# Float32 weights cast in every group of a hybrid encoder block, with first loads in quarters, a fixed TensorE order and a split last pass

## The reference

```python
h = rmsnorm(x, norm1_g);  p = h @ w_in            # 2560 columns: B, C, x~, u, v
y_a = B * conv3(C * x~)                            # causal depthwise, width 3
v = layernorm(v);  y_b = u * (W_s v + b_s)         # 128x128 per head, masked by chunks of 64
y = concat(rmsnorm(y_a), rmsnorm(y_b))
x = x + y @ w_out
a = relu(rmsnorm(x, norm2_g) @ w_up)
x = x + (a * a) @ w_down                           # hidden width 4096
out = rmsnorm(x, final_g)
```

## Time and profile before

| | |
|---|---|
| median of 3 runs | 1398.94 us (1398.16 to 1399.78) |
| profiled execution, its own time | 1400.48 us |
| span on its slowest core (core 2) | 1398.9 us |
| spans of the 8 cores | 1389.2 to 1398.9 us |
| TensorE matmul busy | 1307.5 us, 93% |
| VectorE, ScalarE busy | 657.2 us (47%), 608.9 us (44%) |
| HBM read, written | 138.31 MB, 40.89 MB |

### The profile page before, as it was taken

The page is one execution under the profiler, slowest core; times in us unless marked ns, Lnnn a source line. Parts: engine busy times, 40 slices in busy tenths (PEclk is TensorE's granted clock), DMA queues, the critical chain, the costliest instruction groups (busy, mean ns, idle before and its releaser), DMA issues.

```text
span 1398.9 us, 18098 instructions; the slowest of 8 cores (1389.2 to 1398.9 us)
## 1 busy us (share of the span) xinstructions
PE 1307.5 (93%) x6141; PEld 591.0 (42%) x6264; DVE 657.2 (47%) x1035; ACT 608.9 (44%) x1093; POOL 28.0 (2%) x54
## 2 busy tenths in 40 slices
PE   1789899999999989999999999999999998999995
PEld 0334344444444434444444444444444443444442
DVE  4268831311686953112378883131168694311217
ACT  2444534143465461442556453414346545144152
POOL 1100000000000000000000000000000000000000
PEclk9899999999999999999999999999999999999998
DMA  9999976651271312210255311121125131221003
GB/s 226 174 179 207 194 190 165 140 146 60 95 267 61 121 61 83 99 61 30 82 195 179 148 61 61 60 104 48 61 103 198 61 120 61 82 100 61 1 1 121
DMA packets 39243, 156.26 MB, mean 112 GB/s; under 512 B 2288, under 2 KB 15728, under 8 KB 33520
## 3 DMA queue, kind: packets, MB, share of 16 engines
q1 hardware_dynamic: 20432, 130.98, 26.2%
q0 software_dynamic: 18720, 24.12, 11.9%
HBM read 138.31 MB, written 40.89 MB: 128 GB/s over the span
## 4 chain that ended last, share of the span: by engine, by line
PE 86%; DVE 5%; DMA 5%; issue 2%; ACT 1%; POOL 0%; DVEq 0%; SPq 0%; ACTq 0%; POOLq 0%
PE PS L358 86%; DMA RING<-w_in 4%; DVE HT L449 4%; DMA X<-xT 1%; DVE SACC L437 0%; DVE X L449 0%; ACT SQF L432 0%; DVE ATY L449 0%; ACT RS L417 0%; ACT RS L419 0%; POOL RING L374 0%; DVE YA L561 0%; DVE SSUM L437 0%; DVE X L612 0%; DVE YA L553 0%
## 5 line engine op out<-in xcount | busy, mean ns | idle before, releaser
L358 PE MATMUL PS<-HT,RING 128*128 128x512 bf16 x3005 | 683.8, 383 | 34.0 <-DVE HT L449 19.3
L358 PE MATMUL PS<-ATY,RING 128*128 128x512 bf16 x2509 | 559.3, 379 | 4.9 <-DVE ATY L449 1.5
L358 PEld LDWEIGHTS PS<-HT,RING 128*128 128x128 bf16 x3072 | 300.7, 99 | 399.5 <-issue 48.8
L649 DVE TENSOR_TENSOR X<-PS,X 128x512 f32<-128x512 f32 x256 | 176.2, 691 | 535.7 <-PE PS L358 535.7
L358 PEld LDWEIGHTS PS<-ATY,RING 128*128 128x128 bf16 x2560 | 250.0, 98 | 303.6 <-issue 2.6
L633 ACT ACTIVATE RL<-PS 128x512 f32<-128x512 f32 x256 | 151.6, 596 | 429.7 <-PE PS L358 428.5
L636 ACT ACTIVATE ATY<-RL 128x512 bf16<-128x512 f32 x256 | 158.2, 629 | 19.0 <-ACT RL L633 0.8
L432 ACT ACTIVATE SQF<-X 128x512 f32<-128x512 f32 x168 | 103.2, 626 | 125.5 <-DVE X L612 49.3
L437 DVE TENSOR_TENSOR SACC<-SACC,SQF 128x512 f32<-128x512 f32 x176 | 120.8, 687 | 45.2 <-ACT SQF L432 42.2
L449 DVE SCALAR_TENSOR_TENSOR HT<-X,PRM,RS 128x512 bf16<-128x512 f32 x128 | 86.2, 745 | 53.7 <-ACT RS L419 53.7
L358 PE MATMUL PS<-RING,HT 128*128 128x512 bf16 x252 | 63.6, 404 | 13.1 <-DVE HT L449 12.7
(11 more groups left out here) (58 smaller groups left out, 352.2 us busy)
## 6 DMA issues: line engine op xcount, KB each, us to landing
RING<-sc_up SPq DMA_DIRECT2D x12, 2048.0 KB, 7.9
RING<-sc_dn SPq DMA_DIRECT2D x12, 2048.0 KB, 7.9
X<-xT SPq DMA_DIRECT2D x32, 512.0 KB, 11.8
oT<-X SPq DMA_DIRECT2D x32, 512.0 KB, 4.3
RING<-w_up POOLq DMA_DIRECT2D x4, 2048.0 KB, 20.9
RING<-w_down POOLq DMA_DIRECT2D x4, 2048.0 KB, 21.1
sc_up<-RING SPq DMA_DIRECT2D x4, 2048.0 KB, 9.6
sc_dn<-RING SPq DMA_DIRECT2D x4, 2048.0 KB, 8.9
```

The source lines that it names most:

```text
L358: ins = e.matmul(o, lhsT=l, rhs=r, start=st, stop=sp)
L649: S.add("dve", lambda e, dc=dc, bank=bank: e.tensor_tensor(out=X[xb][:, dc, :], in0=PS[bank][:, :], in1=X[xb][:, dc, :], op=ALU.add), read ...
```

## The change

Weights are cast from float32 by GpSimd's DMA in all four groups; the bf16 copies in HBM, their write-backs and SyncE's reloads are gone. The first casts carry no tokens: V in two halves of 4 k-chunks, then eight quarters of XU and BC in the order of use, then OUT, all queued at once. SyncE sends the parameters, tile 0, and then, behind the first V half, the other small inputs; tile 1 follows behind quarter 2 of BC, and tile mA + 2 behind the first matmul group of `ffn_up(mA, 0)` (a `gate`). TensorE's large groups and GpSimd's casts keep the order of the program (`seq`); statistics matmuls alone are free to move, and have PSUM bank 7 for themselves, so 7 banks rotate. The planner's durations change, and the two rounds behind the first sort by latest start. `stage0` and `norm2` become `x_norm`. V of tile 0 is computed chunk by chunk into 4 banks, its conv stage in two halves with the halo between, and LayerNorm in two halves of two banks. The 2-column copy in `Z` moves from GpSimd to VectorE. `final(mA)` follows `ffn_down(mA, 3)`. In the last group `ffn_down(mA, 3)` and `final(mA)` come before `ffn_up(mB, 3)`, and `tail_down_final` does the last down pass in two halves of 256 tokens, with the sum of squares on ScalarE and TensorE.

```diff
-        order = run(lambda op: (op.prio, -op.bl, op.idx), 0.0)
-        if self.two_pass:
+        order = run(lambda op: (op.prio, op.idx), 0.0)
+        for _round in range(2):
...
-            order = run(lambda op: (ls[id(op)], op.idx), 0.4)
+            order = run(lambda op: (ls[id(op)], op.idx), 0.1)
...
         def alloc_bank():
-            return nxt("bank", 8)
+            return nxt("bank", 7)
+        SBANK = 7
...
-        def load_piece(i, g=1):
-            if g == 0:
-                return cast_piece_to_ring(i)
-            name, sc, src, n = pieces[i]
+        def load_piece(i):
+            src, n = pieces[i]
             slot = i % 4
-            S.add("sp", lambda e, sc=sc, slot=slot, n=n: e.dma_start(out=RING[slot][:, :, 0:n], in_=sc),
-                  reads=[("scr", i)], writes=wk(slot), dma_key=("wl", slot), nbytes=2 * 128 * 8 * n)
+            S.add("pool", lambda e: e.dma_start(out=RING[slot][:, :, 0:n], in_=src), writes=wk(slot),
+                  dma_key=("cast", i), nbytes=4 * 128 * 8 * n, seq=True)
...
+            if m == 0:
+                for k in range(8):
+                    pe_group(banks, [(PS[banks[t]][:, :], HT[:, hm, k, t * 128:(t + 1) * 128], WV[:, k, 0:512],
+                                      k == 0, k == 7) for t in range(4)],
+                             reads=[("HT", hm, k), ("Wq", 0, k // 4)])
...
+        def tail_down_final(m, p):
+            xb, hm = m % 3, m % 2
+            slot_w = (5 + 2 * p) % 4
+            WD = RING[slot_w]
+            HM = MT // 2
+            VS = VH[:].rearrange("p t (u j) -> p (t u) j", u=2)
+            for hf in range(2):
+                lo, hi = hf * HM, (hf + 1) * HM
+                for dc in range(8):
+                    bank = alloc_bank()
+                    pe_group(bank, [(PS[bank][:, 0:HM], WD[:, fc, dc * 128:(dc + 1) * 128],
+                                     AT[:, fc, hm * MT + lo:hm * MT + hi], fc == 0, fc == 7) for fc in range(8)],
+                             reads=[("ATY", fc * 2 + hm) for fc in range(8)] + wk(slot_w))
+                    S.add("dve", lambda e, dc=dc, bank=bank, lo=lo, hi=hi: e.tensor_tensor(
+                        out=X[xb][:, dc, lo:hi], in0=PS[bank][:, 0:HM], in1=X[xb][:, dc, lo:hi], op=ALU.add),
+                        reads=[("ps", bank), ("X", xb, dc)], writes=[("Xh", dc, hf)], n=HM)
+                    S.add("act", lambda e, dc=dc, lo=lo, hi=hi: e.activation(
+                        out=VS[:, dc, :], in_=X[xb][:, dc, lo:hi], func=AF.Square),
+                        reads=[("Xh", dc, hf)], writes=[("VS", dc)], n=HM)
+                for c in range(8):
+                    pe_group(SBANK, [(PS[SBANK][:, 0:HM], ONESD[:, :], VS[:, c, :], c == 0, c == 7)],
+                             reads=[("VS", c), ("const",)], seq=False, slack=0.4)
...
+                for j in range(4):
+                    store_x(m, j, lo, hi, hf)
...
-        for j, (i, q) in enumerate(((2, 0), (1, 2), (1, 0))):
-            cast_quarter(i, q, dur=w0, reads=tokv, tok=toks[j])
...
-        load_x(0)
-        load_x(1, reads=toks)
+        S.add("sp", lambda e: e.dma_start(out=PRM[:, :], in_=prm_d), writes=[("prm",)], dma_key=("misc", 0),
+              nbytes=26624)
+        load_x(0)
+        for kh in range(2):
+            cast_part(0, kh, RING[0][:, 4 * kh:4 * kh + 4, 0:512], pieces[0][0][:, 4 * kh:4 * kh + 4, :],
+                      4 * 128 * 2048)
+        for (i, q) in ((2, 0), (1, 2), (1, 0), (2, 1), (1, 3), (1, 1), (2, 2), (2, 3)):
+            cast_quarter(i, q)
+        load_piece(3)
+        late = [("Wq", 0, 0)]
+        load_x(1, reads=[("Wq", 1, 2)])
...
             for p in range(4):
-                ffn_up(mA, p)
+                ffn_up(mA, p, gate=[("gate", g, p)])
+                if p == 0 and not last:
+                    load_x(mA + 2, reads=[("gate", g, 0)])
+                if last and p == 3:
+                    ffn_down(mA, p)
+                    final(mA)
+                    ffn_up(mB, p)
+                    tail_down_final(mB, p)
+                    continue
                 ffn_up(mB, p)
...
-                if p == 3 and not last:
-                    stage0(mA + 2)
+                if p == 3:
+                    x_norm(mA + 2, G1, gate=[("gate", g, 3)])
                 ffn_down(mA, p)
+                if p == 3:
+                    final(mA)
+                    load_x(mB + 2)
                 ffn_down(mB, p)
```

More of the change, by code:

```diff
@@ L359, in fn @@
                 return ins
-            dur = 0.03 + sum(max(r.shape[-1], 64) for (_o, _l, r, _a, _b) in mms) / 2300.0
-            S.add("pe", fn, reads=reads, writes=[("ps", bank)], dur=dur, prio=prio)
+            dur = sum(0.0025 + max(r.shape[-1], 96) / 2400.0 for (_o, _l, r, _a, _b) in mms)
+            banks = bank if isinstance(bank, list) else [bank]
+            S.add("pe", fn, reads=reads, writes=[("ps", b) for b in banks] + list(gate), dur=dur, seq=seq, slack=slack)
         def wk(slot, qs=(0, 1, 2, 3)):
@@ L379, in save_piece @@
-        def save_piece(i):
-            name, sc, src, n = pieces[i]
-            slot = i % 4
-            S.add("sp", lambda e: e.dma_start(out=sc, in_=RING[slot][:, :, 0:n]),
-                  reads=wk(slot), writes=[("scr", i)], dma_key=("wsave", i), nbytes=2 * 128 * 8 * n)
-        def cast_piece_to_ring(i, dur=None, reads=(), tok=None):
-            name, sc, src, n = pieces[i]
-            slot = i % 4
-            S.add("pool", lambda e: e.dma_start(out=RING[slot][:, :, 0:n], in_=src),
-                  reads=list(reads), writes=wk(slot) + ([tok] if tok else []),
-                  dma_key=("cast", i), nbytes=4 * 128 * 8 * n, dur=dur)
-            save_piece(i)
@@ L393, in load_piece, with cast_part @@
[L393 to L399 removed]
+        def cast_part(i, q, dst, src, nb):
+            S.add("pool", lambda e: e.dma_start(out=dst, in_=src), writes=[("Wq", i % 4, q)],
+                  dma_key=("cast", i, q), nbytes=nb, seq=True)
@@ new lines, in conv_mms @@
+        def conv_mms(m, c, which):
+            hm = m % 2
+            W, off, slot, q = {"C": (RING[1], 512, 1, 2 + c // 2), "X": (RING[2], 0, 2, c // 2),
+                               "B": (RING[1], 0, 1, c // 2)}[which]
+            bank = alloc_bank()
+            pe_group(bank, [(PS[bank][:, :], W[:, k, off + c * 128:off + (c + 1) * 128], HT[:, hm, k, :],
+                             k == 0, k == 7) for k in range(8)],
+                     reads=[("HT", hm, k) for k in range(8)] + wk(slot, (q,)))
+            return bank
@@ L601, in y_norm, with add_to_x @@
             normalize(lambda c: YN[:, mm_, ebase + c, :], lambda c: src[:, c, :], gbase, 4, slot, yk,
-                      [("ATY", mm_ * 8 + ebase + c) for c in range(4)], ())
+                      [("ATY", mm_ * 8 + ebase + c) for c in range(4)])
+        def add_to_x(xb, dc, bank):
+            S.add("dve", lambda e: e.tensor_tensor(
+                out=X[xb][:, dc, :], in0=PS[bank][:, :], in1=X[xb][:, dc, :], op=ALU.add),
+                reads=[("ps", bank), ("X", xb, dc)], writes=[("X", xb, dc)])
         def out_proj(m):
```

503 lines of the change are left out of this document (222 added, 281 removed).

## The result

The changed kernel takes **1408.26 us** (median of 4 runs, 1407.23 to 1408.98) against 1398.71 us for the kernel before in the same comparison (1398.16 to 1399.78): a ratio of **1.0067**, 95% interval 1.0049 to 1.0084. It is slower by 9.5 us where 40 us less were forecast. The profiled execution has a span of 1406.9 us on core 1; the one before had 1398.9 us on core 2.

What follows compares the result with a forecast made beforehand. TensorE, busy 1307.5 of 1398.9 us, was taken as the bound, with its idle, low-clock and end times to win. Terms -10.5 - 10.3 - 3.1 - 14.4 - 2.1 = -40.4 gave 1360.1 profiled, 1359 us median; range 1341 to 1377.

Steps and rivals of the forecast that it cites:

- Casts in every group: Weight loads of all groups: float32 casts arrive in time, hidden in the FFN, XU fitting its 36 us; priced 0.
- rival 3: Group boundaries: XU's casts arrive late and stall each; slower from 49.5 us, 1416 at 55; chance 0.03.
- With that queue free tile 3 lands some 5 us of the 7 earlier.: Boundaries: OUT leaves SyncE's queue, tile 3's norm precedes its need, the 2.18 us wait goes; 4.0 a boundary.
- the -14.4: Three group boundaries together: smaller waits and clock losses, less what a fixed order loses, 3 x -4.8 us.
- The halved entry wait: FFN entry at each boundary: waits of 2.76 and 0.64 us and their clock loss halved, -2.3.
- Rival 1: Only the start pays; boundaries and group 0's FFN entry stay bound by VectorE's amount of work; 1376 us, chance 0.17.
- rival 4: Start: tile 0 lands no sooner because ten queued casts take the share; start gain 5, 1365 us, chance 0.12.
- Start, -10.5.: Before the first large matmul: tile 0 lands at 17.0, V starts at 22.5 instead of 33.06 us; -10.5.
- First stage, 42.5 us.: First token stage: weight and norm waits go, V of tile 1 at 65 instead of 83.88 us; -10.3.
- A statistics bank ... priced 0: PSUM and TensorE order: bank 7 set aside, seven rotating banks cover VectorE for 12 us; cost 0 in the FFN.
- the rest of group 0: Group 0 after its first token stage: of 7.9 us lost, 3.1 saved, for the boundaries' reason; -3.1.
- Tail, -2.1.: End: 9.3 instead of 15.8 us after the last matmul, less added work and two 1.6 us switches; -2.1.

Runs made afterwards that it cites:

- e7: Changed kernel, but OUT's cast at each group's end waits for tile mA's four stores, order replanned; 1376.1 us (die median), -22.2 against the kernel before.
- f1: Changed kernel with every engine's order kept, OUT's cast made to wait for tile mA's stores after planning; 1387.4 us (die median), ratio 0.9948 to before.
- e4: Changed kernel with the halo's square behind tile 0's Exp and two casts to `WST` behind its last scaling; 1403.7 us (die median).
- e1: Kernel before, with GpSimd casting float32 weights in every group and no write-backs; 1404.8 us (die median), ratio 1.0057 to before.
- g1: Changed kernel: OUT's cast behind the stores, tile 0's norm before small inputs' work, tile 1's behind tile 0's convolution, last group's ups first; 1367.8 us (die median).
- e2: Changed kernel, but groups 1 to 3 reload bf16 weights through SyncE from group 0's copies; 1379.9 us (die median), ratio 0.9892 to before.

## Why the prediction was wrong, step by step

- **The step that failed** is in "Casts in every group": the casts were weighed by whether their own weights arrive in time, and "Priced 0". They do arrive: XU and BC in 16.6 us, far from the 49.5 of rival 3; no wait on `RING` stands at a boundary. What they did to SyncE's transfers beside them had no term. The earlier trace rows and the plan itself held both parts: at the start I let a tile load starve casts, at the boundary I did not let a cast stretch a store. Priced at its measured size: the first tile chunk follows the first store by 12.3 us instead of e7's 4.1, and e7 is 35 us faster than the changed kernel, 12 us for each boundary. With the orders held the wait alone is worth 21 us (f1), 7 for each boundary; the rest comes with an order planned for it.
- **"With that queue free tile 3 lands some 5 us of the 7 earlier."** The queue was free, but the change also moved `final(mA)` and its stores behind `ffn_down(mA, 3)`, and tile 3's load behind these stores, as it uses their buffer. With 12.21 and 14.30 us on end it lands at 398.7. And the -14.4 is wrong without the contention too: e7, where tile 3 is in time, gained 1.3 us in three cycles. The halved entry wait did not come (2.48 and 2.66 for 2.76 and 0.64), and 1.46 took the place of 2.18. **Rival 1**, only the start pays, at 1376 and with VectorE as the reason, describes e7 (-22.2, so 1376.5); the forecast took the late load for the whole cause.
- **Rival 3** had the right family, a cast and a SyncE transfer in each other's way, and the wrong victim; it was given 0.03. The same rival at store and load would have asked what a store costs beside a cast, for which the kernel before had no row; the bounds should have said so.
- **Start, -10.5.** Measured -6.5 (26.56). Tile 0 itself came sooner than the 17.0 forecast, ScalarE's last wait for it ends at 12.97, so rival 4 is out. But then ScalarE stood 8.48 us for `xh`, an input that the change had moved behind the first V half; I had taken the small inputs out of tile 0's way without asking who waits for them in front of it. Without that, e4's 19.35 is better than the 22.5 forecast.
- **First stage, 42.5 us.** Measured 51.4 (26.56 to 77.93). Waits are 7.0 of the difference (3.05, 3.03, 0.93); I had left 3. Tile 1 lands at 44.5, not 34: BC's quarter 2, which releases it, landed at 29.0 instead of 26, and a chunk of it issued at 30.20 took 14.32 us beside the queued quarters, where I had given the whole tile 7.8. "A statistics bank ... priced 0" failed here: tile 1's statistics hold bank 7 in written order ahead of tile 0's halo. And I misread the old stage. TensorE's instructions that touch `HT`, in windows up to and from V of tile 1, before and after:

```profile
33.06:83.88 50.82, 31.75 (x126) 0.87 1.00 167
83.88:162.00 78.12, 43.84 (x189) 0.97 1.00 205
```

```profile
26.56:77.93 51.37, 40.84 (x160) 0.90 0.94 143
77.93:145.40 67.47, 35.56 (x161) 1.00 0.62 94
```

- Of the 160 matmuls that I put into the old stage, 32 came only behind it; the records show 126 there and 160 after. They are 6.9 us. So like for like the stage gained 6.4 us (-10.3 forecast) and the rest of group 0, which is 10.7 us shorter, 3.8 (-3.1 forecast: right in size; its reason was not tested).
- **Tail, -2.1.** Right, at -2.5: two switches of 1.67 and 1.56 against 3.3 forecast, and 8.5 us behind the last large matmul (it ends at 1398.45 of 1406.9) against 9.3.

```profile
1353.88 13.97 PE L319 MATMUL PS<-ATY,RING 128*128 128x512 bf16 x64 [1.67 <-ACT ATY L606]
...
1383.44 7.15 PE L319 MATMUL PS<-ATY,RING 128*128 128x256 bf16 x64 [1.56 <-ACT ATY L606]
```

- **The FFN.** TensorE stayed over 99% busy with the casts below it, as forecast:

```profile
1183.00:1350.00 167.00, 166.07 (x770) 75.17 (x769) 36.24 (x53) 59.10 (x97) 3.49 (x4) 1.00 0.33 51
```

- **Left open.** What e1's casts meet in the old order (8.1 us) was not tested by an experiment. Its trace has the loss in the cycles (1001 to 1006 us) and points at the load again: at the first boundary (core 1) OUT's cast is issued 2.1 us behind tile 3's first chunk, the stores ahead of it have their usual 3.2 to 6.3 us, the chunks 8.8 to 12.6, and the cast 31.0. That the wait is worth 35 us with one order and 21 with the other is explained by rows of the first boundary alone. What a still earlier tile 1 would win of g1's 3.11 us was not tried.

## What to carry to other kernels

Price a DMA by what it does to the transfers beside it, not only by when its own data is needed: list for each stretch which transfers run together, and give those on a chain (a store that frees a buffer, the load into it) their worst landing, not their usual one. One wait on one cast, with the order planned for it, turned this change from 10 to 13 us slower to 22 us faster. An order planned on landings should get its landings protected first; and moving one piece of a queue forward only shows the next one behind which it stands, so follow the wait until it stops moving.

## What the runs showed of the hardware

- A 4 MB cast on the software queue beside 512 KB stores and loads on the hardware queue stretched all of them: stores from 4.3 to 12.1 us, the load's chunks at the first boundary from 5.0 to 7.6 (e7) to 10.9 to 14.3, the cast from 16.9 to 28.6. Behind the stores but beside the load (f1) it still took 26.7, behind both (e7) 18.2. The Trainium skill (DMA: Bandwidth & Descriptors, Queues, rings and completion order) says that each DMA engine takes the queues that have work for it in turn, a packet at a time; both being stretched agrees with it. It is not singled out here: e2's stores took 11.8 to 13.7 us too, behind a 2 MB reload in their own queue.
- The rule weighed in rival 3 (same page, SWDGE vs HWDGE vs iDMA), that GpSimd's descriptor writing can be locked out while VectorE runs in its 2-port performance mode, shows no effect here; the rows do not say in which mode VectorE ran: in e7 OUT's cast, issued at 380.22, runs while VectorE is busy 26.77 of 30 us, and OUT's casts land after 18.2 us against 16.9 alone.

```profile
380.00:410.00 30.00, 28.39 (x154) 12.66 (x155) 26.77 (x45) 17.58 (x36) 0.88 (x1) 1.00 0.56 94
```

- Idle time of TensorE costs more than itself: the stretch from 400 to 487 with its waits of 3.64 and 4.04 us was granted a clock of 0.96, part of it at 1.2 instead of 2.4 GHz, against 1.00 from 77.93 to 145.40, whose only wait above a microsecond stands at its very end. Right behind the 4.04, with TensorE busy throughout, it was 0.77, and 16 matmuls ran in 4 us where 20 or 21 run at 1.00.

```profile
77.93:145.40 67.47, 64.99 (x326) 1.00 0.62 94
400.00:487.43 87.43, 77.68 (x391) 0.96 0.54 102
...
420.00:424.00 4.00, 4.00 (x16) 0.77 0.00 0
```
